# The last FFN of a two-block network on one core: gate and value of 18 tiles as seven block products in place of eight

## What is computed

```python
def conv_ffn_2(h, w_up, conv_w, conv_b, w_down):
    a = h @ w_up                                   # (512, 1024) @ (1024, 2 * 2816)
    gate, val = a[..., :D_FF], a[..., D_FF:]
    gp = jnp.pad(gate, ((0, 0), (CONV_W // 2, CONV_W // 2), (0, 0)))
    g = gp[:, 0:L] * conv_w[0] + gp[:, 1:1 + L] * conv_w[1] + gp[:, 2:2 + L] * conv_w[2] + conv_b
    return (jax.nn.silu(g) * val) @ w_down         # (512, 2816) @ (2816, 1024)
```

## Time and profile before

| what | value |
|---|---|
| median of 3 runs | 2865.33 us (2864.4 to 2866.36) |
| the profiled execution | 2864.39 us, span 2862.6 us |
| TensorE busy (products) | 2828.0 us, 99% |
| VectorE / ScalarE / GpSimd busy | 63% / 39% / 15% |
| the last FFN in the span | about 2500 to 2859 us |

### The profile page before, as it was taken

The page is one execution under the profiler, slowest core; times in us unless marked ns, Lnnn a source line. Parts: engine busy times, 40 slices in busy tenths (PEclk is TensorE's granted clock), DMA queues, the critical chain, the costliest instruction groups (busy, mean ns, idle before and its releaser), DMA issues.

```text
span 2862.6 us, 38201 instructions
## 1 busy us (share of the span) xinstructions
PE 2828.0 (99%) x15294; PEld 2370.2 (83%) x15294; DVE 1790.2 (63%) x2575; ACT 1103.3 (39%) x1587; POOL 418.2 (15%) x371
## 2 busy tenths in 40 slices
PE   8999999999999999999999999999999999999999
PEld 5778777888888888888789888889998887788887
DVE  5456557787756677777567787656765347454443
ACT  4233235332343342323445423235554347442322
POOL 0100111786642000000211000000010023100000
PEclk9999999999999999999999999999999999999999
DMA  8344332456648455555224565645553330122222
GB/s 319 132 133 143 101 117 94 158 185 203 229 155 273 169 168 173 166 169 172 93 74 139 167 206 192 193 145 162 177 170 107 125 105 23 60 98 99 98 96 81
DMA packets 124241, 420.12 MB, mean 147 GB/s; under 512 B 21920, under 2 KB 22432, under 8 KB 122400
## 3 DMA queue, kind: packets, MB, share of 16 engines
q1 hardware_dynamic: 102544, 373.15, 39.4%
q0 software_dynamic: 9520, 35.53, 3.8%
q10 hardware_dynamic: 12000, 9.01, 1.0%
HBM read 400.39 MB, written 19.86 MB: 147 GB/s over the span
## 4 chain that ended last, share of the span: by engine, by line
PE 49%; DVE 1%; ACT 1%; issue 0%; DVEq 0%; ACTq 0%
PE bk L112 44%; PE turns L112 3%; PE turns L115 2%; DVE wl L121 0%; ACT wh L118 0%; DVE ctm L133 0%; ACT Pr L118 0%; DVE cpr L121 0%; DVE Q L133 0%; ACT HH L118 0%; DVE HL L121 0%; ACT pr L118 0%; ACT ctm L118 0%; DVE tm L133 0%; ACT L118 0%
## 5 line engine op out<-in xcount | busy, mean ns | idle before, releaser
L121 DVE TENSOR_TENSOR wl<-raw,wh 128x1024 fp32r<-128x1024 f32 x506 | 660.5, 1306 | 404.4 <-ACT wh L118 386.3
L112 PE MATMUL bk<-HH,wh 128*128 128x512 f32 x2176 | 854.1, 393 | 7.3 <-DVE wl L121 4.0
L112 PE MATMUL bk<-HH,wl 128*128 128x512 f32 x2176 | 848.1, 390 | 0.0
L112 PE MATMUL bk<-HL,wh 128*128 128x512 f32 x2176 | 837.5, 390 | 0.0
L118 ACT ACTIVATE wh<-raw 128x1024 fp32r<-128x1024 f32 x506 | 531.6, 1051 | 424.6 <-PE bk L112 420.2
L112 PEld LDWEIGHTS bk<-HH,wh 128*128 128x128 f32 x2176 | 409.0, 188 | 99.2 <-issue 6.5
L112 PEld LDWEIGHTS bk<-HL,wh 128*128 128x128 f32 x2176 | 408.9, 188 | 85.1 <-issue 1.0
L112 PEld LDWEIGHTS bk<-HH,wl 128*128 128x128 f32 x2176 | 408.9, 188 | 84.9
L124 DVE CUSTOM_DVE_ANT_0 ttr<-ar,cB 128x1024 f32<-128x1024 f32 x240 | 307.8, 1283 | 7.6 <-DMA ar<-in_ada_dram 0.3
L112 PE MATMUL bk<-gh,wh 128*128 128x512 f32 x704 | 274.3, 390 | 0.0
L112 PE MATMUL bk<-gh,wl 128*128 128x512 f32 x704 | 274.0, 389 | 0.0
(11 more groups left out here) (398 smaller groups left out, 3740.6 us busy)
## 6 DMA issues: line engine op xcount, KB each, us to landing
raw<-in_wts_dram SPq DMA_DIRECT2D x506, 512.0 KB, 3.5
ar<-in_ada_dram SPq DMA_DIRECT2D x176, 512.0 KB, 4.0
first<-in_adaK_dram SPq DMA_DIRECT2D x8, 1024.0 KB, 20.1
F_d<-CA POOLq DMA_DIRECT2D x8, 512.0 KB, 4.9
E_d<-stg ACTq DMA_DIRECT2D x16, 256.0 KB, 2.4
M_d<-K_d POOLq DMA_DIRECT2D x8, 512.0 KB, 10.6
EB<-E_d POOLq DMA_DIRECT2D x8, 512.0 KB, 6.0
EB<-M_d POOLq DMA_DIRECT2D x8, 512.0 KB, 7.8
```

The source lines that it names most:

```text
L112: return Nothing() if self.e is None else self.e.matmul(*a, **k)
L121: return Nothing() if self.e is None else self.e.tensor_tensor(*a, **k)
```

## The change

In tiles 4 to 21 of the last FFN, gate and value are made together. The 1024 x 256 weights of a tile are seen as two by two blocks of 512 x 128: A11 and A12 (from the first weight unit, the gate's) and A21 and A22 (from the second, the value's), and the 512 tokens as two halves of 256, left and right. Seven block products stand for the eight: three with a block of the weights as it is and four with sums of blocks (S1 to S4), against activations or sums of activations (T, four of them). A part is one such block product: 4 k-blocks x 3 products of 256 columns.

- GpSimd makes S1, S2, S4 and S3 of each tile by additions and subtractions of 128 x 512 (`seven_sums`), into one buffer each, which is free when VectorE has made the low part of the tile before.
- ScalarE and VectorE split each part's weights (sevenh, sevenl; 128 x 512, six buffers, five parts ahead): seven copies and seven subtractions in place of two of each of twice the width.
- The products' sums are taken partly in PSUM by accumulating parts into the same bank, partly by copies on ScalarE (s1, s5, s2) and additions on VectorE (G for the gate's left and right half, vR for the value's right half). `seven_last` puts part A22 of a tile after S1 of the next, or after the fourth k-block of the down product, and it waits for vR (`right`).
- The activations are first added up again from HH and HL (`whole`, into hs), GpSimd makes T from them in tiles 0 to 2, and Th and Tl are its high and low parts.
- The convolution reads G in SBUF, not a PSUM bank. SyncE waits for GpSimd too before it loads a raw buffer of such a tile again.

```diff
+                    if m == 0 and k == 3:
+                        inside()
...
+        v7.NC, v7.AHEAD = 6, 5
...
+        v7.T_OF = {"S1": 0, "S2": 1, "S3": 2, "A22": 3}
...
+        def seven_steps(f, j, j0):
+
+            before = j - 1 if j - 1 >= max(j0, f.seven) else None
+            return before, [("A11", j), ("S1", j)] + ([("A22", before)] if before is not None else []) + [("S2", j), ("A12", j), ("S4", j), ("S3", j)]
...
+        def seven_part(e, f, j, kind, what, start):
+
+            c = v7.c
+            v7.c += 1
+            if not pe.known:
+                v7.list.append((kind, j, base[f.tag, "up", j]))
+                v7.at[kind, j] = c
+            e.wait_ge(*act.of(("sevenh", c)))
+            e.wait_ge(*vec.of(("sevenl", c)))
+            out = BK[seven_bank(j, what)][:, 0:256]
+            for k in range(4):
+                if kind in v7.T_OF:
+                    q = v7.T_OF[kind]
+                    e.wait_ge(*act.of(("Th", k)))
+                    e.wait_ge(*vec.of(("Tl", k)))
+                    xh, xl = v7.Th[:, q, k, :], v7.Tl[:, q, k, :]
+                else:
+                    kk = k if kind == "A11" else 4 + k
+                    t = slice(256, 512) if kind == "S4" else slice(0, 256)
+                    e.wait_ge(*vec.of(("h", f.hn.tag, kk)))
+                    xh, xl = f.hn.hh[:, kk, t], f.hn.hl[:, kk, t]
+                w, lw = v7.h[c % v7.NC][:, k, :], v7.l[c % v7.NC][:, k, :]
+                more = not start
+                e.matmul(out, w, xh, start=(start and k == 0), stop=False, skip_group_check=more)
+                e.matmul(out, w, xl, start=False, stop=False, skip_group_check=more)
+                mm = e.matmul(out, lw, xh, start=False, stop=(k == 3), skip_group_check=more)
+            mm.then_inc(*pe.up(("seven", c), (f.tag, kind, j)))
...
+        def seven_last(e, f, j):
+
+            e.wait_ge(*vec.of(("right", f.tag, j)))
+            seven_part(e, f, j, "A22", "a", False)
+            bank[seven_bank(j, "a")] = (vec, ("pr", f.tag, j))
+
+        def seven_pe(e, f, j, j0, w0):
+            u0 = open_units((f.tag, "up", j), w0, 2)
+            in_sums.update((u0, u0 + 1))
+            before, _ = seven_steps(f, j, j0)
+            claim(e, seven_bank(j, "a"))
+            seven_part(e, f, j, "A11", "a", True)
+            claim(e, seven_bank(j, "c"))
+            seven_part(e, f, j, "S1", "c", True)
+            if before is not None:
+                seven_last(e, f, before)
+            e.wait_ge(*act.of(("s1", f.tag, j)))
+            seven_part(e, f, j, "S2", "a", False)
+            claim(e, seven_bank(j, "b"))
+            seven_part(e, f, j, "A12", "b", True)
+            bank[seven_bank(j, "b")] = (vec, ("left", f.tag, j))
+            e.wait_ge(*act.of(("s5", f.tag, j)))
+            seven_part(e, f, j, "S4", "c", False)
+            bank[seven_bank(j, "c")] = (vec, ("conv0", f.tag, j))
+            e.wait_ge(*act.of(("s2", f.tag, j)))
+            seven_part(e, f, j, "S3", "a", False)
...
+        def seven_high(e, upto):
+            while v7.hi <= min(upto, len(v7.list) - 1):
+                c = v7.hi
+                v7.hi += 1
+                kind, j, u = v7.list[c]
+                src = seven_source(e, c)
+                if c >= v7.NC:
+                    e.wait_ge(*pe.of(("seven", c - v7.NC)))
+                names = {"A12": [("hi", u)], "A22": [("hi", u + 1)]}.get(kind, [])
+                e.activation(v7.h[c % v7.NC][:, :, :].rearrange("p k c -> p (k c)"), src, ACT.Copy).then_inc(*act.up(("sevenh", c), *names))
...
+                e.tensor_tensor(flat(v7.l), src, flat(v7.h).bitcast(F), ALU.subtract).then_inc(*vec.up(("sevenl", c), *names))
...
+        def seven_sums(e, f):
+
+            for i in range(4):
+                e.wait_ge(*vec.of(("hs", i)))
+                if i:
+                    e.wait_ge(*act.of(("Th", i - 1)))
+                    e.wait_ge(*vec.of(("Tl", i - 1)))
+                a, b = v7.hs[i % 2][:, 0, :], v7.hs[i % 2][:, 1, :]
+                left, right = slice(0, 256), slice(256, 512)
+                T = [v7.T[:, q, :] for q in range(4)]
+                e.tensor_tensor(T[0], a[:, right], a[:, left], ALU.subtract).then_inc(*pool.up())
+                e.wait_ge(*pool.now())
+                e.tensor_tensor(T[1], b[:, right], T[0], ALU.subtract).then_inc(*pool.up())
+                e.tensor_tensor(T[2], b[:, right], a[:, right], ALU.subtract).then_inc(*pool.up())
+                e.wait_ge(*pool.now())
+                e.tensor_tensor(T[3], b[:, left], T[1], ALU.subtract).then_inc(*pool.up(("T", i)))
+            S1, S2, S4, S3 = (v7.S[k][:, :] for k in ("S1", "S2", "S4", "S3"))
+            for j in range(f.seven, NF):
+                u = base[f.tag, "up", j]
+                r0, r1 = raw[u % NR], raw[(u + 1) % NR]
+
+                def free(kind):
+                    if j > f.seven:
+                        e.wait_ge(*vec.of(("sevenl", v7.at[kind, j - 1])))
+
+                e.wait_ge(*d_raw[u % NR].of(("w", u)))
+                e.wait_ge(*d_raw[(u + 1) % NR].of(("w", u + 1)))
+                free("S1")
+                e.wait_ge(*pool.now())
+                e.tensor_tensor(S1, r1[:, 0:512], r1[:, 512:1024], ALU.add).then_inc(*pool.up(("S1", j)))
+                free("S2")
+                e.wait_ge(*pool.now())
+                e.tensor_tensor(S2, S1, r0[:, 0:512], ALU.subtract).then_inc(*pool.up(("S2", j)))
+                free("S4")
+                e.wait_ge(*pool.now())
+                e.tensor_tensor(S4, r0[:, 512:1024], S2, ALU.subtract).then_inc(*pool.up(("S4", j)))
+                free("S3")
+                e.tensor_tensor(S3, r0[:, 0:512], r1[:, 0:512], ALU.subtract).then_inc(*pool.up(("S3", j), ("raw", u), ("raw", u + 1)))
...
+            def right():
+                e.wait_ge(*pe.of((f.tag, "S3", j)))
+                e.wait_ge(*act.of(("s5", f.tag, j)))
+                e.tensor_tensor(v7.vR[:, :], out, v7.s5[:, :], ALU.add).then_inc(*vec.up(("right", f.tag, j)))
...
+            def times():
+                e.wait_ge(*act.of(("silu", f.tag, j)))
+                e.wait_ge(*vec.of(("right", f.tag, j)))
+                e.tensor_tensor(p[:, 256:512], g[:, 256:512], v7.vR[:, :], ALU.mult).then_inc(*vec.up())
+                e.wait_ge(*pe.of((f.tag, "A22", j)))
+                e.tensor_tensor(p[:, 0:256], g[:, 0:256], out, ALU.mult).then_inc(*vec.up(("pr", f.tag, j)))
...
+        def seven_vec(e, f, j, j0, bi, last):
+
+            before, steps = seven_steps(f, j, j0)
+            tail = seven_tail_vec(e, f, before, j0) if before is not None else (lambda: None,) * 5
+            b, c = BK[seven_bank(j, "b")][:, 0:256], BK[seven_bank(j, "c")][:, 0:256]
+            for kind, jj in steps:
+                if kind == "A11":
+                    tail[0]()
+                    tail[1]()
+                if kind == "S1":
+                    tail[2]()
+                if kind == "A12":
+                    tail[3]()
+                if kind == "S4":
+                    e.wait_ge(*pe.of((f.tag, "A12", j)))
+                    e.wait_ge(*act.of(("s1", f.tag, j)))
+                    e.tensor_tensor(v7.G[:, 0:256], b, v7.s1[:, :], ALU.add).then_inc(*vec.up(("left", f.tag, j)))
+                if kind == "S3":
+                    e.wait_ge(*pe.of((f.tag, "S4", j)))
+                    e.wait_ge(*act.of(("s2", f.tag, j)))
+                    e.tensor_tensor(v7.G[:, 256:512], c, v7.s2[:, :], ALU.add).then_inc(*vec.up(("conv0", f.tag, j)))
+                    tail[4]()
+                seven_low(e, min(v7.at[kind, jj] + v7.AHEAD, v7.end[f.tag, bi]))
...
+                def inside():
+                    if j0 + n > f.seven:
+                        seven_last(e, f, j0 + n - 1)
+                        v7.end[f.tag, bi] = v7.c - 1
...
+        f3.seven = 4
...
+            seven_sums(e, f3)
...
+                        e.wait_ge(*pool.of(("raw", i)))
```

More of the change, by code:

```diff
@@ L366, in build, with user_before @@
         split = Space()
+        in_sums = set()
+        def user_before(i):
+            i -= NH
+            while i in in_sums:
+                i -= NH
+            return i
         def hi(e, u):
@@ new lines, in seven_vec @@
+        def seven_vec(e, f, j, j0, bi, last):
+            before, steps = seven_steps(f, j, j0)
+            tail = seven_tail_vec(e, f, before, j0) if before is not None else (lambda: None,) * 5
+            b, c = BK[seven_bank(j, "b")][:, 0:256], BK[seven_bank(j, "c")][:, 0:256]
+            for kind, jj in steps:
+                if kind == "A11":
+                    tail[0]()
+                    tail[1]()
+                if kind == "S1":
+                    tail[2]()
+                if kind == "A12":
+                    tail[3]()
+                if kind == "S4":
+                    e.wait_ge(*pe.of((f.tag, "A12", j)))
[7 more added lines that the diff above has]
+                seven_low(e, min(v7.at[kind, jj] + v7.AHEAD, v7.end[f.tag, bi]))
```

(49 more changed lines are left out.)

125 lines of the change are left out of this document (121 added, 4 removed).

## The result

The changed kernel takes 2889.03 us (median of 6 runs, 2887.38 to 2892.55), the kernel before 2865.85 beside it: a ratio of 1.0081, with a 95% interval from 1.0070 to 1.0092. It is 23.2 us slower. The forecast was 2869, with a range from 2854 to 2882.

The account below looks back on a forecast made before the run. TensorE was taken as the bound before, VectorE in changed tiles with sums. Terms -14.4 + 15.8 + 1.0 + 1.0 = +3.4 us on the profiled 2864.39 gave 2867.8; with 0.9 for the median 2868.7, said as 2869, range 2854 to 2882.

Parts of the forecast that it names:

- the sums of the weights: Blocks of seven, seven and four tiles: VectorE, held up by GpSimd's sums, makes TensorE lose +15.8 us together.
- the start: Tiles 0 to 2, with the sums of activations: +1.0 us, between bounds of 0 (all hidden) and 4.
- TensorE per tile: Tiles of seven parts: 84 products at 0.120 us, 10.08 us in place of 10.88; -14.4 us over 18 tiles.
- Who is the bound, and why: In tiles with sums, VectorE, held up by GpSimd's SBUF reads, takes 12.0 us and exceeds TensorE's 10.08.
- the signs named: TensorE idle some 1.9 us once per tile before A22, none in a block's last two; VectorE over 95% busy, GpSimd's sums near 1.7.
- The price per sum: Each GpSimd sum of 512 columns costs VectorE 1.07 us; four cost 4.3, taken as 4.1 beside PSUM readers.
- VectorE's tile of 12.0: A tile with sums: 7.9 us of VectorE's own operations plus 4.1 of being held up, 1.92 over TensorE's 10.08.
- The lead of 2.4 us: First tile of a block: vR ready at 9.1 us, TensorE asks at 11.5, so 2.4 us is off each block's loss.
- The rival that had this place: Start chain stalls: the full 4 us and 3 more in the first seven-part tile, +6 on the forecast, 2875; chance 0.05.
- The clock in the steady tiles: Rival: pauses of about 1.9 us in ten tiles lower the clock; four slow spells give +6 us, 2875; chance 0.08.
- End of a block, ScalarE, DMA: Last gl makes TensorE wait about 0.5 us per block of seven, +1.0; ScalarE under 8.4 of 10.08 us and DMA cost nothing.
- rival of full blocking: Tiles with sums: each GpSimd sum holds VectorE its whole 1.29 us, tile 13.1, total 2881; chance 0.20.

Follow-up runs that it names:

- no_s: The changed kernel without GpSimd's sums of the weights; four parts split a raw block in their place: 2859.03 us, ratio 0.9968.
- no_t: The changed kernel without the sums of activations and their splitting; the four parts take HH and HL: 2881.35 us, ratio 1.0048.
- memset: The changed kernel with each GpSimd weight sum replaced by two memsets of its buffer, all waits kept: 2859.32 us, ratio 0.9977.
- double: The changed kernel with S3 made twice by GpSimd, five sums a tile in place of four: 2908.12 us, ratio 1.0137.
- vecsum: The changed kernel with the weight sums made by VectorE; GpSimd keeps the sums of activations: 2862.79 us, ratio 0.9992.
- gh_late: The changed kernel with ScalarE's high part of a weight part put ahead of gh: 2883.72 us, ratio 1.0061.
- start: The changed kernel with two buffers T, and ScalarE's and VectorE's work on odd sums behind the next tile's weights: 2887.31 us, ratio 1.0074.
- best: The changed kernel with the edits of vecsum, start and gh_late, and VectorE's first low part and sum ahead of tile 3's gate: 2861.36 us, ratio 0.9981.
- all_vec: As best, with VectorE making T too, so GpSimd does nothing in the last FFN: 2862.55 us, ratio 0.9989.

## Why the prediction was wrong

It failed by the size of two terms, the sums of the weights (+15.8 forecast, 30.0 measured by no_s) and the start (+1.0, 7.7 by no_t). Their misses, 14.2 and 6.7, make 20.9, where the table has 19.7 in all; the 1.2 between is within the noise. Of the 14.2, 9.2 are the tile (12 tiles, 0.77 too low each) and 2.9 the leads, as below; the last 2 lie near the first weight sums at the start, and no run tells them apart.

- **TensorE per tile: right.** 10.08 us in no_s, and -14.4 us is what would come if nothing else held.
- **Who is the bound, and why: right.** VectorE, held up by GpSimd's reads, in the tiles with sums; shown by no_s, memset, double and vecsum. Of the signs named, VectorE's share came (96%), and sums of 1.56 to 1.68 us on GpSimd; but TensorE waits twice a tile and not once, and up to the block's last tile (2714.93 and 2718.78). The price per sum was right too: 1.08 in double, 4.2 for four in the timeline, 4.1 forecast. By the full-length rule of the Trainium skill's page "SBUF — State Buffer", section "Who interferes with whom", the four would have cost 5.2; the timeline has 4.2.
- **VectorE's tile of 12.0: the step that failed first.** The working added up durations and left out the gaps; an engine that is full by its sum was taken to have none. The tile was 12.77, of which 0.73 is lost in gaps: 0.3 before convolution steps, which wait for the operation just ahead, and 0.43 behind ScalarE, whose order puts a weight's high part behind gh. gh_late gained that 0.43 in full. Over 5 tiles, the 0.77 between 12.77 and 12.0 are 3.8 us per block of seven.
- **The lead of 2.4 us: too large.** The blocks of seven lost 11.9 and 11.4 us against 10.08 a tile, and 5 x 2.69 less these is 1.5 and 2.1. The block of four had even less: no_t, without the disturbed start, has four waits for pr and vR there, 0.93 + 0.72 + 1.22 + 0.72, with 0.27 on each 4.7 us, where 2 x 2.69 = 5.4. Forecast was a loss of 1.4. The working looked at vR and A22 alone; A11 comes first, and waits for pr.
- **The start: +1.0 forecast, bounds 0 and 4, measured 7.7.** The bounds were wrong, since the sum for VectorE under them was: 10.4 us of new work on 16 in 32.6. The 16 are the steady tile's and leave out the activations that VectorE makes at the FFN's start; the trace of the kernel before has 23.6, so by the working's own sum VectorE was past full (34.0 in 32.6), and 0 was no bound. The working also named GpSimd's 16 sums, but put no price on what they hold VectorE up by, which it had priced for the tiles: 4.6 us in the rows of start, and 2.5 for the first weight sums. Each order tried left a wait near the first seven-part tile: for sevenl in start, for s in best and all_vec. In the profiled execution the clock adds to it: after the 2.46 us TensorE ran 3.5 us at some 0.57, which is 1.5 us lost. The rival that had this place and, with the first seven-part tile, nearly this price got 0.05.
- **The clock in the steady tiles: right** to be kept small. With two waits of 0.7 and 1.2 us in each tile it stayed at 1.00.
- **End of a block, ScalarE, DMA: right.** 0.52 us for gl (0.5 forecast); ScalarE 6.52 of 12.77 us busy. But ScalarE's order counted (gh_late) where its sum did not.

The forecast's rival of full blocking named 2881 for a tile of 13.1. Its tile was nearer than the forecast's, for another reason; its total fell short by the start.

## What to carry to other kernels

A VectorE operation that is moved to GpSimd isn't free when both read SBUF: here a sum of 512 columns costs VectorE 1.08 us if GpSimd makes it and 0.61 if VectorE does. Before giving work away to relieve an engine, price what the giving costs that engine. Where an engine becomes the bound, add to the sum of its durations each wait in its own order, on its own last result and on an engine that stands behind a third one; and look for the first wait of the stalled engine's program, not only for the one that the change writes down. The same block products with the sums on VectorE, and two buffers at the start, beat the kernel before by 0.2%.

## What was not expected of the hardware

- A wait of 0.7 or 1.2 us on TensorE cost 0.27 us more than the profile's bracket: 0.16 ahead of it, where the last product's end lies behind the next one's possible start, and 0.11 behind it, where the first product takes 0.23 us to the next start.
- A memset of 512 columns by GpSimd, 526 ns each, held VectorE up by nothing that shows (688 ns for its subtractions).
- The granted clock did not follow the length of a wait alone. It fell after 2.46 us (0.55 in the window), 3.52 (0.50) and 2.97 (0.50), but stayed at 1.00 after 1.86 us at 2558.74 in the changed kernel and in the window behind the 2.96 us wait of all_vec. Not even the same wait does the same: behind the one for wl in the plain tiles the clock fell in the changed kernel, in double (2.46) and in vecsum (2.42), and stayed up in no_s and memset (2.48) and in gh_late, whose wait and window are these:

```profile
2535.69 0.47 PE L112 MATMUL bk<-HH,wh 128*128 128x512 f32 x1 [2.42 <-DVE wl L121]
...
2536.00:2538.00 2.00, 2.00 (x10) 1.68 (x9) 1.96 (x3) 1.02 (x2) 0.87 (x2) 1.00 0.43 150
```

So the 1.5 us of the start that are the clock's can differ from run to run. What decides is open; no run was made for it.
